# A hybrid decoder layer on eight cores: another planned order, earlier loads, a tail in halves, and identity matmuls in TensorE's expected waits

## The reference, cut to what matters

```python
h = rmsnorm(x, g_pre)
q, k, v, lx, lg = split(h @ w_in)                  # 512, 128, 128, 512, 512 columns
attn = sliding_window_attention(q, k, v, sinks)    # window 128, 8 heads on 2 kv heads, ALiBi, sinks
lru = rg_lru(causal_dwconv(lx, width 4)) * gelu(lg)
x = x + rmsnorm(concat(rmsnorm(attn), rmsnorm(lru)) @ w_out, g_post)
f = causal_dwconv(rmsnorm(x, g_ffn) @ w_up, width 3)   # 2 * 2816 columns
x = x + rmsnorm((gelu(f_gate) * f_value) @ w_down, g_ffn_post)
```

## Time and profile before

| what | us |
|---|---|
| median of 3 runs (799.78 to 809.32) | 801.97 |
| the profiled execution | 802.54 |
| its span on the slowest core (core 2) | 801.0 |
| spans of the eight cores | 792.1 to 801.0 |
| TensorE busy / idle in the span | 709.3 / 91.7 |
| DVE, ACT, POOL busy | 492.5, 379.0, 280.3 |
| mean granted TensorE clock, cores 0 to 7 | 0.954 to 0.961 |

### The profile page before, as it was taken

How to read it: one execution, slowest core, us unless ns; L and a number is a source line. 1 busy time by engine, 2 the same in 40 slices (tenths; PEclk the granted TensorE clock), 3 DMA queues, 4 the chain that set the end, 5 groups by cost and what they waited for, 6 DMA issues and landing times.

```text
span 801.0 us, 11101 instructions; the slowest of 8 cores (792.1 to 801.0 us)
## 1 busy us (share of the span) xinstructions
PE 709.3 (89%) x3636; PEld 325.4 (41%) x3636; DVE 492.5 (61%) x595; ACT 379.0 (47%) x522; POOL 280.3 (35%) x288
## 2 busy tenths in 40 slices
PE   6888848898898965986998899999999999999995
PEld 2343414443353422442544344444444444444442
DVE  4658866966848777655637774322587877873222
ACT  3185695476564867566535442111354544541111
POOL 4027243523542546234534443100144343421000
PEclk9998977998999989998999999999999999999998
DMA  9978124533641425957599443323454445501421
GB/s 169 180 217 268 62 79 132 118 93 47 139 106 27 80 44 93 172 117 154 70 222 176 113 79 53 106 106 124 113 80 80 77 80 79 81 1 44 141 106 53
DMA packets 25112, 85.67 MB, mean 107 GB/s; under 512 B 3040, under 2 KB 3552, under 8 KB 25056
## 3 DMA queue, kind: packets, MB, share of 16 engines
q0 software_dynamic: 12672, 41.20, 32.5%
q1 hardware_dynamic: 12384, 43.77, 16.6%
HBM read 100.98 MB, written 16.78 MB: 147 GB/s over the span
## 4 chain that ended last, share of the span: by engine, by line
PE 63%; DMA 14%; DVE 7%; ACT 6%; issue 6%; POOL 2%; SPq 0%; POOLq 0%; DVEq 0%; ACTq 0%
PE ps L605 62%; DMA ye<-x 5%; DMA wu<-w_up_r 2%; DMA xT<-xT 2%; DMA wc<-w_in_r 2%; DMA out<-ye 1%; DVE thx L904 1%; ACT L576 1%; DVE xc L585 1%; ACT PT L576 1%; ACT a L576 1%; PE ps L609 1%; DVE tv L585 1%; ACT tha L576 1%; POOL wc L148 1%
## 5 line engine op out<-in xcount | busy, mean ns | idle before, releaser
L605 PE MATMUL ps<-h2T,wu 128*128 128x512 bf16 x1408 | 318.9, 387 | 26.0 <-ACT PT L576 7.0
L605 PEld LDWEIGHTS ps<-h2T,wu 128*128 128x128 bf16 x1408 | 138.3, 99 | 197.3 <-issue 41.5
L581 POOL TENSOR_TENSOR u<-tg,tv 128x1024 bf16<-128x1024 f32 x44 | 105.4, 2396 | 138.1 <-DVE tv L581 68.2
L605 PE MATMUL ps<-wdn,u 128*128 128x512 bf16 x704 | 152.4, 379 | 0.0
L585 DVE SCALAR_TENSOR_TENSOR tv<-ps,pp,tv 128x1023 f32<-128x1023 f32 x88 | 112.7, 1280 | 38.7 <-ACT fprev L576 16.3
L585 DVE SCALAR_TENSOR_TENSOR tg<-ps,pp,tg 128x1023 f32<-128x1023 f32 x88 | 112.6, 1280 | 35.6 <-ACT tg L576 21.4
L605 PE MATMUL ps<-hT,wc 128*128 128x512 bf16 x416 | 98.3, 387 | 9.8 <-DVE lx L581 3.8
L605 PEld LDWEIGHTS ps<-wdn,u 128*128 128x128 bf16 x704 | 68.8, 98 | 83.2
L585 DVE SCALAR_TENSOR_TENSOR yf<-ps,st,g 128x1024 f32<-128x1024 f32 x16 | 20.5, 1284 | 108.4 <-POOL st L581 63.7
L591 POOL TENSOR_SCALAR st<-st 128x1 f32<-128x1 f32 (+1 forms) x50 | 15.8, 316 | 178.0 <-ACT yf L576 125.7
L576 ACT ACTIVATE yf<-ps 128x1024 f32<-128x1024 f32 x16 | 16.4, 1023 | 130.0 <-PE ps L605 130.0
(11 more groups left out here) (113 smaller groups left out, 671.5 us busy)
## 6 DMA issues: line engine op xcount, KB each, us to landing
wu<-w_up_r POOLq DMA_DIRECT2D x44, 512.0 KB, 6.2
xT<-xT SPq DMA_DIRECT2D x16, 512.0 KB, 7.5
ye<-x POOLq DMA_DIRECT2D x16, 512.0 KB, 6.6
out<-ye SPq DMA_DIRECT2D x16, 512.0 KB, 3.3
xf<-out SPq DMA_DIRECT2D x16, 512.0 KB, 4.3
out<-xf SPq DMA_DIRECT2D x16, 512.0 KB, 2.7
wdn<-w_down_r POOLq DMA_DIRECT2D x11, 512.0 KB, 10.2
ye<-w_out_r SPq DMA_DIRECT2D x8, 512.0 KB, 7.9
```

The lines of the kernel that those rows point to most:

```text
L581: return P.op(eng, lambda e: e.tensor_tensor(out=AP_(out), in0=AP_(in0), in1=AP_(in1), op=op), reads, writes, dur)
L605: return (lambda e: e.matmul(AP_(out), lhsT=lhsT, rhs=rhs, start=start, stop=stop), tuple(reads), tuple(writes), max(n / 2400.0 + 0.003, 0 ...
```

## The change

What it does:

- The planner: other durations (DVE fixed cost up by 0.03 to 0.035 us, ACT by 0.07, POOL's power down to 0.72), `DMA_RATE` 330e3, a DVE instruction is made longer beside a long POOL instruction, PE matmuls take twice their time after a planned wait of over 2 us until a budget `COLD` is used up. 48 jittered passes of which the best is kept become a chain of 13 passes with fixed keys, each starting from the one before, with jitter in a window of planned time. `place` also returns the planned wait before each PE instruction.
- Loads: `pp` is loaded after the first x tile. The first four weights are as before. Block 1's x has no gate on weights any more and is emitted before weights 5 to 14, each of which is gated by one of block 1's x tiles. `ident`, `wab` and `wxb` are gated by its second tile. w_out also waits for the 12th weight.
- `f_up`: the copy of `fprev` is in one group with the Identity ahead of it.
- `f_down`: squares and the product with the gain in two halves of 512 columns, ahead of 1/root; for tiles 8 to 15 1/root is Ln and Exp on ACT; the scale and the residual are one instruction per half, and each half has its own output DMA.
- Identity matmuls: before a PE instruction that is the first of its PSUM tile, with a planned wait `g` of 0.9 us or more and a planned end of at least 32 us, `emit` first waits for the bank's earlier users and then issues min(int((g - 0.45) / 0.22), 24) matmuls of the identity by itself, four times side by side (512 columns), into the first bank of that tile. The real matmul that follows starts its sum anew, so the results are those of before.

```diff
-DMA_RATE = 300e3
+DMA_RATE = 330e3
+COLD = 3.4
...
+        best = self.place([(o.prio, o.idx) for o in ops])
+        for key in self.PASSES:
+            best = self.place(self.jitter(self.latest(best), key))
+        _, order, fins, banks, extra, self.gaps = best
+        self.extra = extra
...
+            if e == "dve" and dur > 0.4 and port[0] <= t < port[1] - 0.2:
+                dur += 0.25 * (port[1] - t)
+            if e == "pool" and not o.is_dma and dur >= 1.2:
+                port = (t, t + dur)
+            if e == "pe":
+                gaps[i] = t - pe_end
+                if t - pe_end > 2.0:
+                    cold = min(COLD, cold + 0.8 * (t - pe_end))
+                w = min(2 * dur, cold)
+                dur += w / 2
+                cold -= w
+                pe_end = t + dur
...
+    IDLE_MIN, IDLE_MAX = 0.9, 24
+
+    def n_idle(self, o):
+
+        g = self.gaps.get(o.idx, 0.0)
+        if g < self.IDLE_MIN or not o.vps or o.vps[0].ops[0] != o.idx or o.fin < 32.0:
+            return 0
+        return min(int((g - 0.45) / 0.22), self.IDLE_MAX)
...
+                        n_idle = self.n_idle(o) if e == "pe" else 0
+                        if n_idle:
+                            wait_for(self.extra.get(o.idx, set()) | self.idle_deps)
+                            for _ in range(n_idle):
+                                self.idle_mm(eng, o.vps[0])
                         for (fn, _, _, _), deps in zip(o.items, o.deps):
...
+                            wait_for(deps)
                             ins = fn(eng)
...
+            if b == 0 and q_ == 0:
+                P.dma("sp", pp[:], pp_d[:, :], 114688, writes=[pp.k()], slot="pp")
...
-            P.dma("sp", w32[:], wout_d[:, c, :], 524288, reads=[("gate", 1)], writes=[w32.k()], slot=("wo32", c % 3))
+            P.dma("sp", w32[:], wout_d[:, c, :], 524288, reads=[("gate", 1), wc[WORDER[11]].k()], writes=[w32.k()], slot=("wo32", c % 3))
...
-        m1, r1 = stat(1), stat(1)
-        act(yy[:], y.flat(), AF.Square, y.keys(), [st.k("n1", t), yy.k()], 1024, scale=1.0 / 32, accum=sv(m1))
-        rsqrt(r1, m1, 1, [st.k("n1", t)], st.k("nr", t))
-        stt(yy[:], y.flat(), sv(r1), g2[:, 0, :], ALU.mult, ALU.mult, y.keys() + [st.k("nr", t), g2.k(0)], [yy.k()], 1024)
-        tt("dve", xb[:], xb[:], yy[:], ALU.add, [xb.k(), yy.k()], [xb.k()], 1024)
-        P.dma("sp", out_d[tsl, :], xb[:], 524288, reads=[xb.k()], writes=[("out", t)], slot=("xoo", t % 3))
+        m1, r1 = stat(2), stat(1)
+        for dh in range(2):
+            hs = slice(dh * 512, (dh + 1) * 512)
+            act(yq[:], y.flat(dh, 1), AF.Square, y.keys(dh, 1), [st.k("n1", t, dh), yq.k()], 512, scale=1.0 / 32,
+                accum=sv(m1 + dh))
+            tt("dve", yy[:, hs], y.flat(dh, 1), g2[:, 0, hs], ALU.mult, y.keys(dh, 1) + [g2.k(0)], [yy.k(dh)], 512)
...
+            act(sv(m1), sv(m1), AF.Identity, [st.k("n1", t, 0), epsc.k()], [st.k("n1", t, 0)], 1, bias=epsc[:, 0:1])
+            act(sv(r1), sv(m1 + 1), AF.Ln, [st.k("n1", t, 0), st.k("n1", t, 1)], [st.k("nre", t)], 1, bias=sv(m1), tset="N")
+            act(sv(r1), sv(r1), AF.Exp, [st.k("nre", t)], [st.k("nr", t)], 1, scale=-0.5, tset="N")
+        for dh in range(2):
+            hs = slice(dh * 512, (dh + 1) * 512)
+            stt(xb[:, hs], yy[:, hs], sv(r1), xb[:, hs], ALU.mult, ALU.add, [yy.k(dh), st.k("nr", t), xb.k()],
+                [xb.k(dh)], 512)
+            P.dma("sp", out_d[tsl, hs], xb[:, hs], 262144, reads=[xb.k(dh)], writes=[("out", t, dh)], slot=("xoo", t % 3, dh))
...
-            at_(pr, load_xT, b, [wc[WORDER[k]].k() for k in (6, 8, 10, 12)] if b == 1 else ())
...
+    at_(-95, a_norm, 0)
+    at_(-50, load_xT, 1)
+    for n, fc in enumerate(WORDER):
+        if n >= 4:
+            at_(0, load_w, fc, [xTb[min(n - 4, 3)].k()])
+        if n == 5:
+            P.dma("pool", ident[:], id_d[:, :], 65536, reads=[xTb[1].k()], writes=[ident.k()], slot="idb")
+            P.dma("pool", wab[:], wa_d[:, :, :], 262144, reads=[xTb[1].k()], writes=[wab.k()], slot="wab")
+            P.dma("pool", wxb[:], wx_d[:, :, :], 262144, reads=[xTb[1].k()], writes=[wxb.k()], slot="wxb")
...
+    idb = ident[:].rearrange("p (o n) -> p o n", o=1).to_broadcast([128, 4, 128])
+
+    def idle_mm(e, v):
+        e.matmul(ps[:, v.bank, :].rearrange("p (o n) -> p o n", o=4), lhsT=ident[:], rhs=idb, start=True, stop=True)
```

More of the change, by code:

```diff
@@ L161, in schedule, with jitter @@
                 self.succ[d].append(o.idx)
[L162 to L174, removed]
+    def jitter(self, ls, key):
+        ops = self.ops
+        rng = np.random.RandomState(key)
+        sp = (0.5, 1.0, 2.0, 4.0)[rng.randint(4)]
+        w0, w = rng.uniform(-60.0, 480.0), (40.0, 120.0, 700.0)[rng.randint(3)]
+        jit = rng.uniform(-sp, sp, len(ops))
+        return [(o.prio - 1e4 if o.is_dma else ls[i] + (jit[i] if w0 <= ls[i] < w0 + w else 0.0), i)
+                for i, o in enumerate(ops)]
+    def schedule(self):
+        ops = self.ops
+        self.prepare()
+        best = self.place([(o.prio, o.idx) for o in ops])
[3 more added lines that the diff above has]
+        self.extra = extra
         for o in ops:
@@ L183, in latest @@
     def latest(self, got):
-        end, order, fins, _, extra = got
+        end, order, fins, _, extra, _ = got
         ops = self.ops
@@ L246, in place @@
         dmat = {"sp": 0.0, "pool": 0.0}
-        SETS = {"T": ("T", None), "N": ("N", None)}
+        port = (0.0, 0.0)
+        cold, pe_end, gaps = COLD, 0.0, {}
         def ready(o):
@@ L394, in place @@
         return (max(o.fin for o in ops), order, [o.fin for o in ops],
-                {v.vid: v.bank for v in self.vps.values()}, extra)
+                {v.vid: v.bank for v in self.vps.values()}, extra, gaps)
+    IDLE_MIN, IDLE_MAX = 0.9, 24
[4 more added lines that the diff above has]
+        return min(int((g - 0.45) / 0.22), self.IDLE_MAX)
     def emit(self):
@@ L432, in body, with wait_for @@
                     waited = {}
+                    def wait_for(deps):
+                        need = {}
+                        for j in deps:
+                            p = ops[j]
+                            if p.is_dma:
+                                key = ("s", p.slot)
+                            else:
+                                if p.eng == "pe" and e == "pe":
+                                    continue
+                                key = ("e", p.eng)
+                            if p.val > need.get(key, 0):
+                                need[key] = p.val
+                        for key, v in need.items():
+                            if waited.get(key, 0) >= v:
+                                continue
+                            waited[key] = v
+                            sem = ssem[key[1]] if key[0] == "s" else esem[key[1]]
+                            eng.wait_ge(sem, v)
@@ L433, in body @@
                     for o in order[e]:
                         ins = None
-                        for (fn, _, _, _), deps in zip(o.items, o.deps):
[L436 to L452, removed]
+                        n_idle = self.n_idle(o) if e == "pe" else 0
@@ L569, in act @@
         ptr = sum(not isinstance(v, (int, float)) for v in (scale, bias))
-        dur = 0.11 + 0.00083 * n + 0.093 * ptr + (0.19 if accum is not None else 0.0)
+        dur = 0.18 + 0.00083 * n + 0.093 * ptr + (0.19 if accum is not None else 0.0)
         def fn(e):
@@ L586, in stt @@
                                                             in1=AP_(in1), op0=op0, op1=op1),
-                    reads, writes, 0.17 + n / 960.0)
+                    reads, writes, 0.205 + n / 960.0)
     def ts(eng, out, in0, s1, s2, op0, op1, reads, writes, n, fast=1):
-        dur = 0.14 + n / fast / 960.0 if eng == "dve" else 0.28 + n * 0.0013
+        dur = 0.175 + n / fast / 960.0 if eng == "dve" else 0.28 + n * 0.0013
         return P.op(eng, lambda e: e.tensor_scalar(out=AP_(out), in0=AP_(in0), scalar1=s1, scalar2=s2,
@@ L1138, in f_up @@
             gk = g.keys()
-            act(t_[:], g.flat(), AF.Identity, gk + PPK, [t_.k()], 1024, scale=fw(ch, 2), bias=fb(ch))
+            items = [(lambda e, t_=t_, g=g, ch=ch: e.activation(out=t_[:], in_=g.flat()(), func=AF.Identity,
+                                                                scale=fw(ch, 2), bias=fb(ch)),
+                      tuple(gk + PPK), (t_.k(),), 1.21)]
             if hf == 0:
-                act(fprev[:, ch, :], g.at(lambda p: p[:, 1, 510:512]), AF.Copy, gk, [fprev.k(ch)], 2)
+                items.append((lambda e, g=g, ch=ch: e.activation(
+                    out=fprev[:, ch, :], in_=g.at(lambda p: p[:, 1, 510:512])(), func=AF.Copy, scale=1.0, bias=0.0),
+                    tuple(gk), (fprev.k(ch),), 0.17))
+            P.group("act", items)
             fl = g.flat()
@@ L1180, in f_down @@
         xb, yy = F_["xf"][t % 3], F_["yf"][t % 2]
```

(11 more changed lines are left out.)

30 lines of the change are left out of this document (18 added, 12 removed).

## The result

The changed kernel takes 805.66 us against 799.78 (9 runs each): ratio 1.0069, interval 1.0046 to 1.0092. Measured again in the third batch of experiments it is 1.0053 (1.0027 to 1.008). I had forecast 788 us, 1.7% faster. It is 0.5 to 0.7% slower.

What follows compares the result with a forecast made beforehand. TensorE's dense stretch from 447.62 us was fixed; only 81.9 us of earlier waits, half-clock matmuls and the 9.6 us tail could give. 802.5 - 2.8 - 5 - 10 + 4 = 788.7, said as 788 us, range 780 to 796.

Steps and rivals of the forecast that it cites:

- Order (-10): New planner's order before the dense stretch: a sixth less of about 65 us idle, -10 us, bounds +8 and -25.
- loads (-5): Block 1's x loaded ahead of weights 5 to 14: about half of 11 us won, -5 us, bounds -11 and +5.
- +5 if half of the 10.5 shows: Bad bound of the loads step: weights and constants moved past come up to 10.5 us later; half showing costs 5.
- Identity matmuls, +4: Before 447.62 us: 24 us added, 4 hidden, half of 20 passed on (+10), clock gives 6 back; bounds -16 and +40.
- 35 to 45: Clock sign: half-clock stretches would sum to some 35 to 45 us, the 20 us one gone or short.
- Rival B: Identity matmuls between bank release and first real matmul are paid in full, up to 40 us less 6: 818.7 us; chance 0.08.
- Its bar, 17.8 us of other gains: Gains forecast for tail, loads and order; rival B decides from 24 us of identity matmuls on the chain (17.8 + 6).
- Rival C: Order and loads give nothing, the DVE, ACT and DMA chain being as long in any order: 803.7 us; chance 0.14.
- A: Identity matmuls fit data waits or long-free banks, cost nothing and give 6 us: 778.7 us; chance 0.32.
- Tail, -2.8: After the last matmul: only half the columns late (2.3 us less), last DMA halved (0.5); -2.8 us, between -1.5 and -4.
- The forecast start of the dense stretch, 436: Sign: dense stretch starts at about 436 us instead of 447.6; 450 or later with over 200 identity matmuls means B.
- My sign for C, other waits of 80 us: Sign for rival C: waits other than identity ones still sum to 80 us.

Runs made afterwards that it cites:

- third batch of experiments: The changed kernel run once more, unedited, against the kernel before: 1.0053.
- batch 4: Against the kernel before, on one chip: changed kernel without identity matmuls 0.9953; old order and loads with the new tail 0.9965.
- batch 1: Against the kernel before, on one chip: changed kernel without identity matmuls 0.9989; old order and loads with the new tail 0.9948.
- the 88: The changed kernel without the 24 identity matmuls of its longest planned wait, the other 88 kept in 14 places: 1.0043 of the kernel before.
- batch 2: The kernel before, with its own order, loads and tail, plus 93 identity matmuls in 13 places by the same rule: 1.0109.
- the 24 of the longest wait alone: The changed kernel with identity matmuls only before a scores tile of block 1 (planned wait over 7 us): 0.9942 of the kernel before.
- the 24 of the data part: The changed kernel with identity matmuls only for planned waits after the bank is free, 24 in 6 places: 0.9984 of the kernel before.
- early eight places: The changed kernel with only the 47 identity matmuls in 8 places planned before 150 us, longest run left out: 1.0003 of the kernel before.
- The doubled kernel: The changed kernel with twice as many identity matmuls in the same places, 224: 1.0248 of the kernel before.
- first kernel without identity matmuls: The changed kernel with the identity matmul limit of 24 set to 0, same order: 0.9989 of the kernel before.

## Why the prediction was wrong, point by point

- **Order (-10) and loads (-5) are the steps that failed.** With the new tail on both sides, the new order and loads measure 0.9953 against 0.9965 in batch 4 and 0.9989 against 0.9948 in batch 1: -1 us known to some 3 us and +3 known to some 4, for my -15. (The regrouped fprev copy, forecast at nothing, is in this comparison and was not run by itself.) I had taken "a sixth of the idle time" with no row behind it, which the text itself said.
- The loads step was wrong in place too. x of block 1 did go early, but then a weight was late: PE waits 5.2 us for `wc` (the list of PE's waits above), where before it waited 1.05. In the first 50 us PE is busy 33.45 us, against 39.09 before, and by 100 us it has not made that up: 366 matmuls of which 14 are identity ones, against 390. The order differs too, so not all of this is the loads. It was my "+5 if half of the 10.5 shows". That block 1's units would cover it was wrong, as they need the same weights.

PE first in these windows, after, and then before:

```profile
0.00:50.00 50.00, 33.45 (x117) 14.60 (x118) 23.23 (x65) 12.27 (x21) 10.29 (x25) 0.93 0.97 206
50.00:100.00 50.00, 44.40 (x249) 21.60 (x246) 31.74 (x44) 32.85 (x49) 17.20 (x13) 0.97 0.53 163
```

```profile
0.00:50.00 50.00, 39.09 (x169) 17.83 (x170) 29.92 (x74) 17.64 (x30) 10.31 (x25) 1.00 0.93 179
50.00:100.00 50.00, 39.88 (x221) 17.58 (x220) 37.05 (x50) 34.58 (x53) 24.42 (x15) 0.93 0.58 179
```

- **Identity matmuls, +4:** measured +5 to +9 us, same sign, under-sized. The count was 112 (24 us estimated, 24.3 at full clock), and their place behind the bank's release as forecast. Half let through was near the 40% of the 88. What I had wrong is the gain. I gave 6 us back, as identity matmuls would prevent the one half-clock stretch of 20 us. They did not: the changed kernel has a longer one, which holds the wait of 6.0 us and reaches into the 24 that come behind it. In the old order (batch 2) the matmuls behind the long wait did run at full clock, but started 3.2 us later. This stretch in the changed kernel, PE alone:

```profile
112.80:136.30 23.50, 15.18 (x53) 0.50 0.33 113
```

- One step behind this gain was the kind of wait. I had read the longest one as a data wait in full; 2.7 of its 6.4 us were for the bank (batch 2), and in the new order the longest is ended by DVE's last read of the bank. Filling it alone (24 matmuls) won nothing that can be told from none. The half-clock time outside the tail is about 52 us, against 61, and not 35 to 45; in the kernel without identity matmuls (batch 4) it is about 79. The 52 and 79 are worked out from the slowest core's mean granted clock, 0.966 over 804.5 us and 0.949 over 801.7, less the tail.
- Rival B had the right place and the right sign, and too high a price: the matmuls were not paid in full, but by some 40%. Its bar, 17.8 us of other gains, was never there: with only the tail's 3 to 4 us won, 5 to 9 us were enough to turn the sign.
- Rival C, 803.7, was the nearest in time: order and loads nothing, identity matmuls +4. I gave it 0.14. Its cause is what the experiments found: the order and the loads gave nothing. A is out: the part of the planned waits after the bank's release holds 24, not 112.
- Tail, -2.8: 9.6 to 5.8 us in the trace and -2.8 to -4.2 by measurement. Right. With -1 to +3 for order and loads and +5 to +9 for the identity matmuls the parts come to about 0 to +9, and +4 to +6 was measured. The last lines of the tail:

```profile
798.68 0.60 ACT L613 ACTIVATE yq<-ps 128x512 bf16<-128x512 f32 x1 [3.67 <-PE ps L642]
...
799.46 0.59 ACT L613 ACTIVATE st<-st 128x1 f32<-128x1 f32 x2
...
800.29 1.41 DVE L622 SCALAR_TENSOR_TENSOR xf<-yf,st,xf 128x512 f32<-128x512 f32 x2
```

From the last Square to the last add it is 3.0 us (2.9 forecast); Ln and Exp took 0.59 together, not 0.38, and the hops were shorter.

- The forecast start of the dense stretch, 436, came out at 455. By my own list, "at 450 or later" meant B, whose other sign (over 200 identity matmuls) did not come. My sign for C, other waits of 80 us, did not come either (68.8 - 27.1 = 41.7 us), though C was nearest. Such lists should test one cause each.

The best kernels are those with the new tail, and with the 24 of the longest wait alone, the 24 of the data part, or none: 0.994 to 0.999. What stays open: why the two planners' best orders tie, although the newer has somewhat longer durations, nearer to the trace; how far the loss lies behind bank waits; and which of the early eight places cost the 4 us.

## What to carry to other kernels

Dummy work can fill only the part of a wait in which the engine may already write; a wait for the buffer itself can't be filled through that buffer, and dummy work put behind it is work, of which some 40% reached the end time here. Even where it cost nothing it won nothing that could be measured. Before pricing it, split every wait by what ended it. And give a new order, of which only the code is known, a gain of zero with a wide range: here two good orders tied, and planning anew with other loads, another planner or other keys moved the time by 1.2 to 1.8%.

## What I had not expected of the hardware

- Higher clock, longer time. The doubled kernel had mean granted clocks of 0.971 to 0.985 and was the slowest of all, 1.0248; the fastest had 0.955 to 0.964.
- A third level of the granted clock. In the profiled execution of the first kernel without identity matmuls, cores 6 and 7 (one die) ran parts of the first 210 us at 0.81, and ended 806.1 and 799.4 us after their start, the six others at 785 to 798. Cores 4 and 5 of the same die had 1.00 between 162 and 200 us. Core 6, PE alone:

```profile
162.00:200.00 38.00, 37.18 (x213) 0.81 0.40 82
```

That is the 13/16 of the Trainium skill ("TensorE: Matmul & The Clock Gate", section "The HAM clock gate (the 'warmup' mystery)"), of which I had said that the trace does not agree. It does not in the 344 us dense stretch of any profiled execution here; but the level exists, in this one execution, on two cores of a die, where the page has the whole die at it while the load lasts.
- The plan's end is 751 or 759 us where the chip takes 800, yet in three pairs of plans, each by one planner, the one with the lower end was the faster (751 and 761, 759 and 767, 759 and 772), and the second pair's difference, 7.7 us planned, came out at 11 to 14 us. Across changes of the program or the planner it told nothing: 772 with the old loads measured 1.0112 and 767 with the new ones 1.0132, whose intervals overlap, and 751 by the old planner tied with 759 by the new.
